# Norm scales behind the projections, cross attention by head and half, a tile border with one pass of weights and x, square sums shared with GpSimd

## The reference, cut to what matters

```python
def rms_norm(t, g):
    return t * rsqrt(mean(t * t, axis=-1) + 1e-6) * g

h = rms_norm(x, g_mix)
q, k, v, cu, cb, cc, gl = split(h @ w_in)      # 1024, 256, 256, 3 x 1024, 4096
y_attn = windowed_gqa_sink(rope(q), rope(k), v, sink) @ w_attn_out  # 8 heads of 128, 2 kv heads, |i-j| <= 128
y_conv = (cb * short_conv_centred(cc * cu, conv_w)) @ w_conv_out    # depthwise, 3 taps
g_a, g_c = split(sigmoid(gl + b_gate))
x = x + (g_a * y_attn + g_c * y_conv) @ w_o
x = x + memory_cross_attention(rms_norm(x, g_cross), rms_norm(mem, g_mem), w_cq, w_ckv, w_co)  # 4 heads of 128
hf = rms_norm(x, g_ffn)
x = x + (silu(hf @ w_gate) * (hf @ w_up)) @ w_down                  # width 5632
return rms_norm(x, g_final)
```

## Time and profile before

| | |
|---|---|
| median of 3 runs | 3952.4 us (lowest 3952.3) |
| the profiled execution, its own time | 3957.9 us |
| its span on the slowest core | 3956.8 us |
| PE busy | 3535.8 us, 89% |
| DVE, ACT, GpSimd busy | 1210.2, 625.6, 286.2 us |
| DMA | 344 MB moved, 601.5 MB read from HBM |

### The profile page before, as it was taken

The page is one execution under the profiler, slowest core; times in us unless marked ns, Lnnn a source line. Parts: engine busy times, 40 slices in busy tenths (PEclk is TensorE's granted clock), DMA queues, the critical chain, the costliest instruction groups (busy, mean ns, idle before and its releaser), DMA issues.

```text
span 3956.8 us, 45501 instructions; the slowest of 8 cores (3947.6 to 3956.8 us)
## 1 busy us (share of the span) xinstructions
PE 3535.8 (89%) x16425; PEld 1616.8 (41%) x16750; DVE 1210.2 (31%) x2101; ACT 625.6 (16%) x1271; POOL 286.2 (7%) x545
## 2 busy tenths in 40 slices
PE   5788999996899999999527889999967999999997
PEld 2444444442344444444204344444423444444443
DVE  3756222245411101102336662212454011011015
ACT  2134211114200000001200342111142000000011
POOL 0100000000000000001000000000000000000010
PEclk7899999997899999999768999999988999999998
DMA  7753444661344444446855333445613444444458
GB/s 170 127 85 51 72 78 75 120 126 22 59 75 76 79 75 77 78 75 102 158 118 121 68 59 65 75 78 101 130 32 53 75 77 79 75 77 78 75 88 178
DMA packets 115995, 344.40 MB, mean 87 GB/s; under 512 B 12992, under 2 KB 17472, under 8 KB 115776
## 3 DMA queue, kind: packets, MB, share of 16 engines
q0 software_dynamic: 77904, 276.89, 42.6%
q1 hardware_dynamic: 37872, 64.58, 5.6%
HBM read 601.50 MB, written 16.78 MB: 156 GB/s over the span
## 4 chain that ended last, share of the span: by engine, by line
PE 83%; DVE 6%; DMA 4%; issue 3%; ACT 3%; SPq 0%; DVEq 0%; ACTq 0%
PE ps L304 83%; DMA arena<-xT 4%; DVE arena L322 3%; ACT arena L319 3%; DVE arena L330 1%; DVE arena L326 1%; DVE arena L333 1%; PE ps L307 0%; SPq L345 0%; DVEq L144 0%; DVE arena L336 0%; ACTq L144 0%; ACT L319 0%; SPq L144 0%; DVE arena L339 0%
## 5 line engine op out<-in xcount | busy, mean ns | idle before, releaser
L304 PE MATMUL ps<-arena 128*128 128x512 bf16 (+3 forms) x15929 | 3509.4, 379 | 383.8 <-DVE arena L322 285.0
L304 PEld LDWEIGHTS ps<-arena 128*128 128x128 bf16 (+1 forms) x16254 | 1587.1, 99 | 2287.3 <-issue 526.4
L322 DVE TENSOR_TENSOR arena<-ps,arena 128x512 f32<-128x512 f32 (+4 forms) x950 | 597.7, 658 | 2183.6 <-PE ps L304 2142.3
L345 POOL DMA_DIRECT2D arena<-wp x540 | 285.3, 529 | 3630.8 <-PE ps L304 3514.0
L319 ACT ACTIVATE arena<-ps 128x512 f32<-128x512 f32 (+5 forms) x378 | 216.8, 628 | 1681.4 <-PE ps L304 1676.0
L319 ACT ACTIVATE arena<-arena 128x512 f32<-128x512 f32 (+4 forms) x482 | 279.3, 587 | 965.2 <-DVE arena L322 635.9
L322 DVE TENSOR_TENSOR arena<-arena 128x512 f32<-128x512 f32 (+3 forms) x457 | 252.0, 557 | 303.5 <-ACT arena L319 279.6
L330 DVE SCALAR_TENSOR_TENSOR arena<-arena 128x512 bf16<-128x512 f32 (+4 forms) x320 | 228.7, 767 | 181.8 <-DMA arena<-xT 93.6
L319 ACT ACTIVATE arena<-ps,arena 128x512 f32<-128x512 f32 (+1 forms) x210 | 122.4, 617 | 629.7 <-PE ps L304 591.6
L326 DVE TENSOR_SCALAR arena<-arena 128x384 bf16<-128x384 f32 (+3 forms) x241 | 70.8, 345 | 29.8 <-DMA arena<-small 19.3
L307 PE MATMUL ps<-arena 128*128 128x128 bf16 x496 | 38.8, 225 | 20.0 <-ACT arena L319 12.3
(11 more groups left out here) (3 smaller groups left out, 0.3 us busy)
## 6 DMA issues: line engine op xcount, KB each, us to landing
arena<-wp POOLq DMA_DIRECT2D x412, 512.0 KB, 6.2
arena<-xT SPq DMA_DIRECT2D x160, 256.0 KB, 13.0
arena<-wp POOLq DMA_DIRECT2D x64, 480.0 KB, 5.6
arena<-wp POOLq DMA_DIRECT2D x64, 448.0 KB, 8.3
outT<-arena SPq DMA_DIRECT2D x64, 256.0 KB, 3.8
arena<-cs SPq DMA_DIRECT2D x4, 576.0 KB, 9.3
arena<-memT SPq DMA_DIRECT2D x16, 128.0 KB, 6.5
arena<-xT SPq DMA_DIRECT2D x16, 64.0 KB, 6.0
```

The lines of the kernel that those rows point to most:

```text
L304: pr.add("pe", lambda e: e.matmul(out, lhsT, rhs, start=start, stop=stop), reads=[lhsT, rhs], writes=[out])
L322: pr.add("dve", lambda e: e.tensor_tensor(out, in0, in1, op), reads=[in0, in1], writes=[out])
L345: return pr.add(q, lambda e: e.dma_start(out=out, in_=in_), reads=list(sb_reads), writes=list(sb_writes), is_dma=True)
```

## The change

1. **Scales behind the projections.** `hT` is x times gain, cast to bf16 (`cast`, on ACT, DVE or GpSimd), without `rstd`. The scale is applied to what comes out: in the rotary tables, in v's copy (a column of scales, from the new `columns`, which turns the square sums into one number per partition), in cu's copy (`rstd2`) and once more behind the conv, before both sigmoids, in the exp of cross attention, and before and behind the silu.
2. **Square sums shared.** `Stat` keeps up to two partial sums, one added up by DVE and one by GpSimd. GpSimd also takes rotary's last sum, the scaling of P, and products in the conv and in the FFN.
3. **Cross attention by head and half.** The unit is now one head and one half, not four heads and 128 tokens, and the query projections stand between the units.
4. **Tile border.** In tile 0 the last pass of `down` does both halves with one load of the weights; x of the next tile is read once, through a ring of eight chunks, and both cast into `hT` and squared (`x_use`, three chunks per output chunk). The finals follow in `qkv_next`.
5. **Start and memory.** Casts instead of the first norm; both halves use one load of the k and v weights; the memory's projections move into `conv_attn` (`mem_part`).
6. **Weight loads.** The program is generated twice. The first pass gives the list of pieces; in the second, `wfree` issues the load of the piece six further on right behind the last use.

The diff, leaving out the changed indentation, names of areas, and parts that repeat a pattern:

```diff
+    def cast(dst, src, gi, c, eng):
+        if eng == "act":
+            act(dst, src, AF.Copy, scale=gain(gi, c))
+        else:
+            ts(dst, src, gain(gi, c), ALU.mult, eng)
+    class Stat:
...
+        def add(self, src, eng):
+            dst = self.parts[eng]
+            if eng not in self.begun:
+                self.begun.add(eng)
+                act(dst, src, AF.Square)
+                return
+            s = self.slots[self.n % len(self.slots)]
+            self.n += 1
+            act(s, src, AF.Square)
+            tt(dst, dst, s, ALU.add, eng)
+    SQ2 = [sq[:, 0, :], sq[:, 1, :]]
+    SQ4 = SQ2 + [sq2[:, 0, :], sq2[:, 1, :]]
+    def finish(accs, dst, n=HW):
+        b = balloc()
+        for i, a in enumerate(accs):
+            mm(bank(b)[:, 0:n], onesF, a, i == 0, i == len(accs) - 1)
...
+    def columns(accs, nblk, dst, bias=None):
+        b = balloc()
+        for n in range(nblk):
+            for i, a in enumerate(accs):
+                mm(bank(b)[:, n:n + 1], a[:, n * 128:(n + 1) * 128], onesF[:, 0:1], i == 0, i == len(accs) - 1)
...
     def rope(src, N, col0, out, blocks=False):
-        tt(out, tA, tB, ALU.add)
+        tt(out, tA, tB, ALU.add, "pool")
+    def qkv_first():
+        for c in range(16):
+            dma_x(xT[:, 0, c, :], c, 0, HW)
+            if c == 1:
+                wissue(); wissue()
+        load_cs(0)
+        wissue(xT[:, 0, 11, :]); wissue(xT[:, 0, 15, :])
+        for c in range(16):
+            dma_x(xT[:, 1, c, :], c, HW, HW)
+        wissue(xT[:, 1, 3, :]); wissue(xT[:, 1, 7, :])
...
+        for c in range(16):
+            cast(hT[:, 0, c, :], xT[:, 0, c, :], 0, c, "dve")
+            st0.add(xT[:, 0, c, :], "dve" if c % 2 else "pool")
+        wk = [wF(("in", 8)), wF(("in", 9))]
...
+        vb = v_blocks(wv, 0, [tok(0, e) for e in range(4)], list(range(4)))
+        finish(st0.accs(), rstd[:, 0, :])
+        columns(st0.accs(), 4, rcol[:, 0:4])
+        rope_tables(0, HW, rstd[:, 0, :])
...
+        for n in (2048, 1024, 512, 256):
+            tt(mf[:, 0:n], mf[:, 0:n], mf[:, n:2 * n], ALU.add, "pool")
+        finish([mf[:, 0:256]], rstdM, NMEM)
     def conv_attn(it):
-                    ts(Pb[:, sl, h, 0:nk], Sb[:, sl, h, 0:nk], st_r[:, s4, h:h + 1], ALU.mult)
+                ts(Pb[:, sl, h, 0:nk], Sb[:, sl, h, 0:nk], st_r[:, s4, h:h + 1], ALU.mult, "pool")
-                    act(cuS[:, sl, hf * HW:(hf + 1) * HW], bank(bu[hf]), AF.Copy)
+                tt(cuS[:, sl, hf * HW:(hf + 1) * HW], bank(bu[hf]), rstd2[:, hf, :], ALU.mult)
+            for hf in range(2):
+                tt(ca[:, hf * HW:(hf + 1) * HW], ca[:, hf * HW:(hf + 1) * HW], rstd[:, hf, :], ALU.mult, "pool")
+            if it == 0:
+                mem_part(j)
     def out_proj(it):
-            for c in range(12):
+        for c in range(16):
+            b = proj2(wF(("o", c)), lambda hf: lambda k: mT[:, hf, k, :])
+            wfree()
+            for hf in range(2):
+                x = resid(b[hf], c, hf)
+                cast(hT[:, hf, c, :], x, 1, c, "act")
+                sts[hf].add(x, "dve" if c % 2 else "pool")
     def cross(it, sts):
+        units = [(h, hf) for hf in range(2) for h in range(4)]
+        def co(hf, q):
+            for c in range(4 * q, 4 * q + 4):
...
+                x = resid(b, c, hf)
+                cast(hT[:, hf, c, :], x, 2, c, "pool" if c % 2 else "act")
+                new[hf].add(x, "pool" if c % 4 == 0 else "dve")
+        P_(0)
+        for hf in range(2):
+            columns(sts[hf].accs(), 4, rq[:, 0, 4 * hf:4 * hf + 4], lnS)
+        P_(1); S_(0)
+        P_(2); S_(1)
+        P_(3); T_(0); S_(2)
+        P_(4); T_(1); S_(3); V_(0)
...
+        P_(7); T_(4); S_(6); V_(3)
+        T_(5); S_(7); V_(4)
+        co(0, 0)
+        V_(5); T_(6)
+        co(0, 1)
...
     def ffn(it, sts):
         def act_mul(bg, bu, jj, hf):
-                act(s, bank(bg), AF.Silu)
+            tt(s, bank(bg), rstd[:, hf, :], ALU.mult)
+            act(s, s, AF.Silu)
+            tt(s, s, rstd[:, hf, :], ALU.mult, "pool")
+        def x_use(n):
+            for _ in range(n):
+                if xu[0] < 32:
+                    c, hf = order[xu[0]]
+                    s = ring[xu[0] % 8]
+                    xu[0] += 1
+                    cast(hT[:, hf, c, :], s, 0, c, "act")
+                    nst[hf].add(s, "pool")
+                    x_issue(1)
+            elif not last:
+                fst = [Stat({"dve": acc[:, hf, :]}, SQ2) for hf in range(2)]
+                for c in range(16):
+                    b = proj2(wF(("down", fg, c)), lambda hf: rest[hf], KC=nb)
+                    wfree()
+                    for hf in range(2):
+                        x = resid(b[hf], c, hf)
+                        fst[hf].add(x, "dve")
+                    done = xu[0] == 32
+                    x_use(3)
+                    if xu[0] == 32 and not done:
+                        for hf in range(2):
+                            finish(nst[hf].accs(), rstd[:, hf, :])
+                            columns(nst[hf].accs(), 4, rcol[:, 4 * hf:4 * hf + 4])
+                        load_cs(it + 1)
```

More of the change, by code:

```diff
@@ L161, in piece_keys @@
         lst.append(("ck", m))
-    for q in range(4):
-        lst.append(("cv", q))
+    for h in range(4):
+        lst.append(("cv", h))
     for q in range(2):
@@ L390, in finish_rstd @@
[L390 to L411 removed]
+        keys = generate(nc, arena, ps, ARENA, x_d, mem_d, wp_d, small_d, cs_d, cst_d, out_d, None)
@@ new lines, in qkv_first @@
+        vb = v_blocks(wv, 4, [tok(1, e) for e in range(4)], list(range(4, 8)))
+        finish(st1.accs(), rstd[:, 1, :])
+        columns(st1.accs(), 4, rcol[:, 4:8])
+        rope_tables(HW, HW, rstd[:, 1, :])
+        for g in range(2):
+            rope(bank(b1[g]), HW, HW, kT[:, g, HW:T])
+            bfree(b1[g])
+        v_out(vb)
+        bh = balloc()
+        for g in range(2):
+            for k in range(16):
+                mm(bank(bh)[:, g * 128:(g + 1) * 128], wk[g][:, k, :], hH[:, k, :], k == 0, k == 15)
@@ L887, in build_program @@
-        for it in range(NT):
-            if it == 0:
-                qkv_first()
-                mem_stage()
-            else:
-                qkv_next(T * it, finals)
-            conv_attn(it)
-            mix(it)
-            out_proj(it)
-            cross(it)
-            finals = ffn(it)
-        pr.emit(es, out_dmas)
-    return nc
+                        b = proj(wF(("down", fg, c)), rest[hf], KC=nb)
+                        wfree()
+                        x = resid(b, c, hf)
+                        st[hf].add(x, "dve" if c % 2 else "pool")
@@ L901, in _F @@
+    fin = []
+    for it in range(NT):
+        if it == 0:
+            qkv_first()
+        else:
+            qkv_next(T * it, fin)
+        conv_attn(it)
+        mix(it)
+        sts = out_proj(it)
+        sts = cross(it, sts)
+        fin = ffn(it, sts)
+    if keys is None:
+        return seen
+    assert freed[0] == len(seen) == len(keys)
+    return pr, out_dmas
 def _F(W, m, KC, k0=0):
```

1233 lines of the change are left out of this document (645 added, 588 removed).

## The result

| | before | after |
|---|---|---|
| times | 3952.4, 3952.3 us | 3739.5, 3736.7, 3738.2 us |
| ratio, 95% interval | | 0.9458, 0.9431 to 0.9485 |
| span profiled | 3956.8 us | 3738.4 us |

The median of all four times of the changed kernel is 3738.8 us. The forecast was 3717 us in 3640 to 3840: 22 us, 0.6%, too low.

The account below looks back on a forecast made before the run. TensorE, busy 89% of the span at nearly full clock, was taken as the bound, so only its holes could be won. Terms summed to −235 us: 3957.9 becomes 3723, the median 5.5 lower, 3717; range 3640 to 3840.

Parts of the forecast that it names:

- the 2 us set aside for mix and FFN: Mix and FFN: added DVE and GpSimd operations price nothing, the double statistic costs 2 us.
- the start's term of the sum: Start: x in earlier, casts replace the norm, GpSimd's sums wait behind loads; attention at about 168 instead of 200, −32 us.
- The tree's wait: Start: PE waits 14 us for GpSimd's tree of the memory's square sums, behind the last rope.
- GpSimd's price: Elementwise work on GpSimd: 1.2 us for 512 columns, 0.95 us for 384; ends 0.692 and 1.753 us.
- Dear and shared: Rival, chance 0.17: GpSimd operations of 1.75 us, or DVE's and GpSimd's sums in each other's way; 3825 us.
- Attention and conv: Tile 0 takes in the memory projections, +2 us; tile 1's seven waits shrink as P's scaling moves to GpSimd, −10 us.
- Cross attention: Each tile: projections between score steps cover the chain, output chunks stay at 2.2 us; 122 against 162 us, −40 us.
- Border: Tile border: one pass over the down weights, x no longer last, ACT–GpSimd chain last; 109 against 225 us, −116 us.
- The single wait at the statistic: Border: PE waits once, 26 us, at the statistic, as a chunk's chain takes 7.7 us against PE's 6.1.
- The price of transfers: Border before: a weight piece and up to three x chunks take 5.8 us of DMA per 3.0 us PE needs.
- Tail: End of kernel: 16 final DVE operations, 10.7 us, are split and the statistic doubles; −1 us.
- The rival by which x still lands last at the border: Border, chance 0.11: x lands late even in one pass, PE's statistic waits with it, half the gain goes; 3775 us.

Follow-up runs that it names:

- the deferred sum: Changed kernel with VectorE's square sum of a cross-attention output chunk issued behind the next chunk's residual sum: 3699.2 us, ratio 0.933.
- queries all ahead of the scores: Changed kernel with all eight cross-attention query projections ahead of the first score, as in the kernel before: 3773.2 us, ratio 0.953.

## Why the prediction was right or wrong, point by point

- **The total** was 3738 for 3717, and the sum of the gains 218 for 235. Short of it were the start by 13.5 us, cross attention by 8 and the two conv stages by 3.5; border and tail gave 6 more, and the 2 us set aside for mix and FFN didn't show.
- **The step that failed** is the start's term of the sum: −32 us in the prediction, −18.5 measured, which is 13.5 of the 17 us by which the gains fell short. Attention's scores were to begin at about 168 us and began at 184.8.
- **Start** (32 forecast, 18.5 measured). The mechanism was as read: sums behind waiting loads, PE standing until then. Its times were too short. The queue was free at 45.2 us and the first sum ran at 46.2, where the prediction had "≈ 41": the DMA engines were busy for 96% of the first 50 us, and which transfer took the 4 us more isn't separated. A pair of chunks took 2.2 to 2.4 us, not 2.0, beside GpSimd's sums, where DVE's first sum took 1.33 us and its casts 0.94 us each instead of 0.48: casts ended at 61.7 us, not 52, which is 10 us. The second half's casts ended at 100.7 us, not 85, so that some 6 us more were lost there, where DVE's sums from SBUF took 1.3 to 1.75 us. The tree's wait was 15.3 us for 14.
- **GpSimd's price**: 1.2 us taken for a sum, 1.29 measured; 0.95 taken for the scaling of P with 384 columns, 1.30 measured (0.93 is the price with 256). The Trainium skill (GPSIMD Engine Reference, Performance versus the Vector engine) made of 0.692 us an estimated 1.36: nearer than mine for a sum. Its rule to keep such work off GpSimd did not hold for the whole: with all of it on VectorE the kernel is 34 us slower, although its start is 30 us faster.
- **Dear and shared**: of its two alternatives the second, engines in each other's way, was there. The first, operations of 1.75 us, was not, but for the 32 casts of 1.73 us. Pairs of sums from SBUF do stand in each other's way (0.69 to 1.33 us, 0.16 to 3.08 us). The rule of the Trainium skill (SBUF: State Buffer, Who interferes with whom), one read port held for a whole instruction, agrees with the trace: DVE's sums with an operand in PSUM kept their 0.686 us. The rival's price was too high; most of DVE's sums have that operand (854 of 512 columns in fp32, against 142 without), which would explain it, but no run separates it.
- **Attention and conv** (+2 and −10 forecast, +2.8 and −7.3 measured). In tile 1 PE's seven waits for DVE, 28.2 us, became 17.4 us, about the 10 forecast, and five new ones for GpSimd's scaling, which the prediction put at nothing, took 4.3 us. The weight loads in GpSimd's queue were hidden as read.
- **Cross attention** (40 each; 37 and 35). A chunk at 2.2 us forecast, 2.19 measured; the prediction's terms for four chunks, 0.6, 2.8, 2.8 and 2.2, add up to 8.4 and not 8.2 us, so that its own sum gives 2.3. PE's waits in front of transposes, 5.0 us in tile 0, were put at nothing. That this chain was untouched by the change was right, and the deferred sum shows what it cost, 17 us in each tile.
- **Border** (116; 118). The single wait at the statistic was forecast at 26 us and ended by the chain of ACT and GpSimd: 31.2 us, named GpSimd's. A chunk took 8.7 us (the pattern returns after 34.8 us for four) where 7.7 was taken. The price of transfers, 5.8 us of DMA in 3.0 us of PE work in the first half, was right in kind, but only half of it: weights were worth 54 us, the second reading of x 63 on top, and the latter, as its trace reads, by SP's order more than by its bytes. The prediction had no step for that; its total was made from the stage after, not from the parts removed. A period 1 us longer and a wait 5 us longer than taken should have left less than 116 us, and yet 118 were gained: other terms, which weren't taken apart, were off the other way, and that the total fits within 2 us is in part luck.
- **Tail**: 5 for 1; the split between the two engines wasn't taken apart further.
- The rival by which x still lands last at the border is out: ACT, GpSimd and DVE there waited for each other or for PE, never for x, and PE waited once, for GpSimd's sum.

## What to carry to other kernels

Where engines run in the order written down, look for what stands behind an instruction that waits: a waiting load, a statistic, a sum held for another engine's square. Each of the three was worth 17 to 37 us here by being moved a few lines; the rewrite of the start gained 18.5. Before work goes to a second elementwise engine, ask which operands both read. In attention, conv and cross attention, where VectorE mostly has an operand in PSUM, the hand-over was worth 14 to 18 us a stage; at the start, where both read SBUF, it was worth nothing (175.2 against 174.7 us). That the operands are the reason is argued from the lengths of single operations. And when a stage has two kinds of transfers, cut out one after the other: the small one may wait in a queue and cost more than the large one.

## What the runs showed of the hardware

- A DVE addition of 128x4 from SBUF took 3.08 us in place of 0.16 beside a GpSimd addition of 2048 columns, and a GpSimd sum of 512 columns 3.25 us in place of 1.26 beside DVE's tree. ACT's exps in that stretch kept their 0.5 us. The addition of 3.08 us ended at 178.0 us; the tree's first step, 4.49 us in the changed kernel, ran from 173.5 to about 178.0. In the changed kernel's cross attention, sums of 512 columns with an operand in PSUM took 0.68 us beside GpSimd too.
- A GpSimd cast of 512 columns to bf16 took 1.73 us, longer than its sum of the same columns with two inputs, 1.29 us. I had expected the reverse.
- GpSimd's cost for 256, 384 and 512 columns of `tensor_scalar` (0.93, 1.30, 1.73 us) is close to proportional.
- With gaps of 0.64 us in front of single transposes (queries all ahead of the scores), TensorE's granted clock was 0.53 of full over 30 us of cross attention. The changed kernel, with projections between the transposes, had 1.00 from 880 to 905 us and 0.83 from 905 to 935.
